# Feed-forward passes 1 to 9: the low parts of the weights move to GpSimd

## What is computed

```
f = rms_norm(h, ffn_norm_pre)
f = (silu(f @ w_gate) * (f @ w_up)) @ w_down      # w_gate, w_up: 2048 x 5632, w_down: 5632 x 2048
h = h + rms_norm(f, ffn_norm_post)
```

## Time and profile before

| | |
|---|---|
| median of three runs | 1993.66 us |
| span of the profiled execution, first to last instruction | 1992.0 us |
| time of the profiled execution beyond its span | not listed; 1.66 us lie between the span and the median |
| PE busy | 1979.0 us, 99% |
| PE weight load busy | 1681.0 us, 84% |
| DVE busy | 1668.8 us, 84% |
| ACT busy | 1147.6 us, 58% |
| POOL busy | 18.9 us, 1% |
| mean DMA rate | 198 GB/s |

### The profile page before, as it was taken

The page is one execution under the profiler, slowest core; times in us unless marked ns, Lnnn a source line. Parts: engine busy times, 40 slices in busy tenths (PEclk is TensorE's granted clock), DMA queues, the critical chain, the costliest instruction groups (busy, mean ns, idle before and its releaser), DMA issues.

```text
span 1992.0 us, 29428 instructions
## 1 busy us (share of the span) xinstructions
PE 1979.0 (99%) x10149; PEld 1681.0 (84%) x10149; DVE 1668.8 (84%) x2336; ACT 1147.6 (58%) x1482; POOL 18.9 (1%) x37
## 2 busy tenths in 40 slices
PE   9999999999999999999999999999999999999998
PEld 8888888888888888998888888888888888888886
DVE  7788888889888868767777787999999988888887
ACT  6666566666655545565545565556555555555575
POOL 0000000000000000000000000000000000000000
PEclk9999999999999999999999999999999999999999
DMA  8666676666566566545556667666566666766754
GB/s 235 200 191 190 190 206 184 188 192 195 172 207 209 189 203 223 156 132 156 191 191 239 205 207 242 189 202 202 190 201 200 200 201 201 254 201 207 244 189 152
DMA packets 255197, 394.74 MB, mean 198 GB/s; under 512 B 28840, under 2 KB 161440, under 8 KB 252928
## 3 DMA queue, kind: packets, MB, share of 16 engines
q1 hardware_dynamic: 251104, 369.87, 59.7%
q0 software_dynamic: 3824, 23.43, 3.5%
q10 hardware_dynamic: 176, 0.20, 0.0%
HBM read 387.08 MB, written 6.36 MB: 198 GB/s over the span
## 4 chain that ended last, share of the span: by engine, by line
PE 98%; DVE 1%; ACT 0%; DMA 0%; issue 0%; DVEq 0%; SPq 0%; ACTq 0%
PE acc L655 16%; PE acc L851 15%; PE acc L853 15%; PE acc L852 15%; PE acc L660 8%; PE acc L912 6%; PE acc L913 6%; PE acc L914 6%; PE acc L1107 1%; PE acc L785 1%; PE acc L637 1%; PE acc L636 1%; PE acc L638 1%; PE acc L1038 1%; PE acc L1242 0%; PE acc L714 0%
## 5 line engine op out<-in xcount | busy, mean ns | idle before, releaser
L1914 DVE TENSOR_TENSOR wlo<-raw,whi 128x1024 fp32r<-128x1024 f32 (+2 forms) x559 | 662.5, 1205 | 110.8 <-ACT whi L1351 108.3
L1351 ACT ACTIVATE whi<-raw 128x1024 fp32r<-128x1024 f32 (+1 forms) x560 | 572.2, 1044 | 244.4 <-PE acc L853 81.7
L655 PE MATMUL acc<-u,whi 128*128 128x512 f32 x1376 | 328.7, 391 | 0.0
L851 PE MATMUL acc<-whi,u 128*128 128x512 f32 x824 | 323.0, 392 | 0.1
L853 PE MATMUL acc<-whi,u 128*128 128x512 f32 x824 | 320.8, 389 | 0.0
L852 PE MATMUL acc<-wlo,u 128*128 128x512 f32 x824 | 320.6, 389 | 0.0
L655 PEld LDWEIGHTS acc<-u,whi 128*128 128x128 f32 x1376 | 252.7, 188 | 48.8
L851 PE MATMUL acc<-whi,g 128*128 128x512 f32 x520 | 202.8, 390 | 0.1
L853 PE MATMUL acc<-whi,g 128*128 128x512 f32 x520 | 202.4, 389 | 0.0
L852 PE MATMUL acc<-wlo,g 128*128 128x512 f32 x520 | 202.3, 389 | 0.0
L1374 ACT ACTIVATE whi<-raw 128x1024 fp32r<-128x1024 f32 x72 | 76.5, 1062 | 209.9 <-PE acc L914 162.0
(11 more groups left out here) (597 smaller groups left out, 2990.8 us busy)
## 6 DMA issues: line engine op xcount, KB each, us to landing
raw<-w_in_in SPq DMA_DIRECT2D x208, 512.0 KB, 3.8
raw<-w_gate_in SPq DMA_DIRECT2D x176, 256.0 KB, 3.0
raw<-w_up_in SPq DMA_DIRECT2D x176, 256.0 KB, 3.3
raw<-w_down_in SPq DMA_DIRECT2D x88, 512.0 KB, 4.6
raw<-w_ssm_o_in SPq DMA_DIRECT2D x64, 512.0 KB, 4.3
raw<-w_in_in SPq DMA_DIRECT2D x64, 256.0 KB, 4.0
raw<-w_attn_o_in SPq DMA_DIRECT2D x32, 512.0 KB, 4.7
raw<-w_out_in SPq DMA_DIRECT2D x32, 512.0 KB, 4.9
```

Source lines behind the costliest of these rows:

```text
L655: return T.matmul(bank(banks[i]), wh[:, j, i * P:i * P + P], src[:, kts[j], :, :].rearrange("p a s -> p (a s)"), start=start and j == 0, s ...
L851: T.matmul(o, x_hi, wh[:, j, :], start=start, stop=False, skip_group_check=True)
L1351: S.activation(whi[:, slot, 0:w], raw[:, slot, 0:w], ACT.Copy).then_inc(sem("hi_ready"), 1)
L1914: V.tensor_tensor(wlo[:, slot, 0:w], raw[:, slot, 0:w], whi[:, slot, 0:w].bitcast(F32), ALU.subtract) \
```

## The change

It touches passes 1 to 9 of `ff`.

- All low parts of raw weights are made by GpSimd (`raw_low`, `seven_raw_low`): one instruction of 128x1024 for a plain chunk, three of 128x512 for a pair, the first of which counts a new semaphore, `first_lo`. `lo_ready` is counted by GpSimd in these passes. At the end of pass 9 VectorE waits for the last of them before it makes the low parts of pass 10.
- VectorE does nothing for a plain chunk. For a pair (`pooled_sums`) it makes the three sum instructions and the two low parts of the sums.
- TensorE starts a pair at `first_lo`, waits for the second and third low part later, and does the product with the last raw block after two of the products with sums.
- ScalarE has two more waits ahead of the high parts of the sums (`t_used`, and one on `chunk_done` that applies only to adjacent pairs, of which this order has none). The high part of a `dn` operand moves from chunk 12 to chunk 1 of the next pass; on VectorE its sums move from chunk 11 to chunk 15, its low part from chunk 14 to chunk 1 of the next pass.
- SP waits for the sums too before it overwrites a slot of a pair, and its loads of all 11 passes are written out, with no loop.
- Several semaphores are merged under one name, in this phase and in others, with the same order of events. Lists for passes with four or five pairs are added and left empty.

```diff
+FF_FOURS = ()
+FF_FIVES = ()
+POOLED = tuple(("ff", _j) for _j in FF_THREES)
...
 # SP, load
                 sp.wait_ge(sem("lo_ready"), num(phase, it, c) - RING + 1)
+                if phase == "ff" and isinstance(it, int):
+                    it_, c_ = (it, c - RING) if c >= RING else (it - 1, c - RING + PHASES["ff"][0])
+                    if is_pooled("ff", it_) and is_seven("ff", it_, c_):
+                        n = SEVENS_BEFORE["ff", it_] + SEVEN["ff", it_].index(pair_of("ff", it_, c_))
+                        sp.wait_ge(sem("t_sum"), 3 * n + (3 if c_ % 2 else 1))
...
 # GpSimd, behind the store of h to h_dram
+        def raw_low(it, c):
+            slot = c % RING
+            pool.wait_ge(sem("hi_ready"), num("ff", it, c) + 1)
+            G.tensor_tensor(wlo[:, slot, :], raw[:, slot, :], whi[:, slot, :].bitcast(F32), ALU.subtract) \
+                .then_inc(sem("lo_ready"), 1)
+        def seven_raw_low(it, c):
+            slot = c % RING
+            pool.wait_ge(sem("hi_ready"), num("ff", it, c) + 1)
+            G.tensor_tensor(wlo[:, slot, 512:], raw[:, slot, 512:], whi[:, slot, 512:].bitcast(F32), ALU.subtract) \
+                .then_inc(sem("first_lo"), 1)
+            G.tensor_tensor(wlo[:, slot + 1, 0:512], raw[:, slot + 1, 0:512], whi[:, slot + 1, 0:512].bitcast(F32),
+                            ALU.subtract).then_inc(sem("lo_ready"), 1)
+            pool.wait_ge(sem("hi_ready"), num("ff", it, c + 1) + 1)
+            G.tensor_tensor(wlo[:, slot + 1, 512:], raw[:, slot + 1, 512:], whi[:, slot + 1, 512:].bitcast(F32),
+                            ALU.subtract).then_inc(sem("lo_ready"), 1)
+        pool.wait_ge(sem("lo_ready"), num("ff", FF_THREES[0], 0))
+        for it in FF_THREES:
+            for c_ in range(16):
+                if not is_seven("ff", it, c_):
+                    raw_low(it, c_)
+                elif c_ % 2 == 0:
+                    seven_raw_low(it, c_)
...
 # TensorE, seven_products
-            begin(phase, it, c + 1)
+            if pooled:
+                pe.wait_ge(sem("first_lo"), pooled_before(it, n) + 1)
+            else:
+                begin(phase, it, c + 1)
...
             product(v_bank(phase, it, 0), tokens(t0 + 2 * p, 0), weights(slot, 1), first, last)
-            product(c_bank(phase, it, 1, 0), tokens(t0 + 2 * p + 1, 0), weights(slot + 1, 1))
+            if pooled:
+                begin(phase, it, c)
+            else:
+                product(c_bank(phase, it, 1, 0), tokens(t0 + 2 * p + 1, 0), weights(slot + 1, 1))
...
+            if pooled:
+                begin(phase, it, c + 1)
+                product(c_bank(phase, it, 1, 0), tokens(t0 + 2 * p + 1, 0), weights(slot + 1, 1))
             pe.wait_ge(sem("t_lo"), 2 * done + 2)
...
 # VectorE
+        def sums_low(phase, it, n, half):
+            t, t_hi, t_lo = sums_at(phase, it), thi[phase], tlo[phase]
+            dve.wait_ge(sem("t_hi"), 2 * n + 1 + half)
+            two = slice(2 * half, 2 * half + 2)
+            V.tensor_tensor(t_lo[:, two, :], t[:, two, :], t_hi[:, two, :].bitcast(F32), ALU.subtract) \
+                .then_inc(sem("t_lo"), 1)
+        def pooled_sums(phase, it, c, between=None):
...
+            V.tensor_tensor(t[:, 0:2, :], raw_f[:, inner].rearrange("p (a n) -> p a n", a=2),
+                            raw[:, slot, 0:512].unsqueeze(1).to_broadcast([P, 2, 512]), ALU.add) \
+                .then_inc(sem("t_sum"), 1)
...
+            V.tensor_tensor(t[:, 2, :], t[:, 0, :], raw[:, slot + 1, 0:512], ALU.add).then_inc(sem("t_sum"), 1)
+            dve.wait_ge(sem("t_sum"), 3 * n + 2)
+            V.tensor_tensor(t[:, 3, :], t[:, 2, :], raw[:, slot + 1, 512:], ALU.add).then_inc(sem("t_sum"), 1)
+            if between:
+                between()
+            sums_low(phase, it, n, 0)
+            if not ahead:
+                sums_low(phase, it, n, 1)
...
-            if not is_seven(phase, it, c):
+            if is_pooled(phase, it):
+                if is_seven(phase, it, c) and c % 2 == 0:
+                    pooled_sums(phase, it, c, between)
+            elif not is_seven(phase, it, c):
                 split(phase, it, c)
```

More of the change, by code:

```diff
@@ L83 @@
 SEVEN["pg", 0] = (0, 1)
-SEVEN.update({("ff", _j): (0, 1, 2) if _j in FF_THREES else (0, 1) for _j in range(1, FF_LAST + 1)})
+SEVEN.update({("ff", _j): tuple(range(5 if _j in FF_FIVES else 4 if _j in FF_FOURS else 3 if _j in FF_THREES else 2))
+              for _j in range(1, FF_LAST + 1)})
 SEVEN.update({("dn", _j): (0, 1, 2, 3, 4, 5, 6, 7, 8) for _j in range(2)})
@@ L93, with pairs_in @@
 }
+PAIRS.update({("ff", _j): (5, 6, 0, 1, 2, 3, 4, 7) for _j in FF_FIVES})
+PAIRS.update({("ff", _j): (4, 5, 0, 1, 6, 2, 3, 7) for _j in FF_FOURS})
+def pairs_in(phase, it):
+    return PAIRS.get((phase, it), PAIRS[phase]) if isinstance(it, int) else PAIRS[phase]
 PAIRS_AT = {"so": 16, "ao": 16, "wo": 0, "ff": 0, "dn": 0, "pg": 0}
-MERGE = {_p: PAIRS_AT[_p[0]] + 2 * PAIRS[_p[0]].index(SEVEN[_p][-1]) + 2 for _p in PASSES}
+MERGE = {_p: PAIRS_AT[_p[0]] + 2 * pairs_in(*_p).index(SEVEN[_p][-1]) + 2 for _p in PASSES}
 SEVENS_BEFORE = {_p: sum(len(SEVEN[_q]) for _q in PASSES[:_i]) for _i, _p in enumerate(PASSES)}
@@ L140, in is_seven, with is_pooled, pooled_before @@
     return (phase, it) in PASSES and pair_of(phase, it, c) in SEVEN[phase, it]
+def is_pooled(phase, it):
+    return isinstance(it, int) and (phase, it) in POOLED
+def pooled_before(it, n):
+    return sum(len(SEVEN["ff", _j]) for _j in FF_THREES if _j < it) + n
 def num(phase, it, c):
@@ L295, in build, with sums_at @@
         s_u[ph] = at("s_u_" + ph, [P, 2, 512], hi_at)
+    ts_ff = at("ts_ff", [P, 4, 512], G0 + 32 * 2048)
+    def sums_at(phase, it):
+        return ts_ff if phase == "ff" and isinstance(it, int) and it in FF_APART else tr[phase]
     raw_f, whi_f, wlo_f = (w[:, :, :].rearrange("p r n -> p (r n)") for w in (raw, whi, wlo))
@@ L546, in _ @@
             first = 0
-            if its == 1 or phase in TURNS or phase == "ssm":
+            if its == 1 or phase == "ssm":
                 for c_ in range(per):
@@ L550, in _ @@
                 first = 1
-            if its > 1:
+            if phase == "ff":
+                for it_ in range(its):
+                    for c_ in range(per):
+                        load(it_, c_)
+            elif its > 1:
                 with sp.Fori(first, its) as it:
@@ L924, in seven_products @@
                 pe.wait_ge(sem("ff_lo"), FF_LAST + 1)
-            product(v_bank(phase, it, 3), differences(3) if phase in KEPT else tokens(2 * p, 1), sums(1), first, last)
+            product(v_bank(phase, it, 3), differences(3) if phase in KEPT else tokens(2 * p, 1), sums(1), first, last) \
+                .then_inc(sem("t_used"), 1)
+            if pooled:
+                begin(phase, it, c + 1)
+                product(c_bank(phase, it, 1, 0), tokens(t0 + 2 * p + 1, 0), weights(slot + 1, 1))
             pe.wait_ge(sem("t_lo"), 2 * done + 2)
@@ L1378, in seven_high @@
             for half in range(2):
+                if is_pooled(phase, it) and half == 0:
+                    act.wait_ge(sem("t_used"), n)
+                if is_pooled(phase, it) and half and is_seven(phase, it, c - 1):
+                    act.wait_ge(sem("chunk_done"), num(phase, it, c))
                 act.wait_ge(sem("t_sum"), 3 * n + 1 + 2 * half)
                 two = slice(2 * half, 2 * half + 2)
-                S.activation(thi[phase][:, two, :], tr[phase][:, two, :], ACT.Copy).then_inc(sem("t_hi"), 1)
+                S.activation(thi[phase][:, two, :], sums_at(phase, it)[:, two, :], ACT.Copy).then_inc(sem("t_hi"), 1)
         def wide_high(phase, it, c, between=None):
@@ L1809, in _ @@
                     ff_gate(it - 1)
[L1810 to L1811 removed]
+                if c_ == 1 and 2 <= it <= 5:
+                    operand_high(DN_OPERANDS + it - 2)
         act.wait_ge(sem("p_in"), 64)
@@ L2155, in tables @@
                     link(last)
-            last.then_inc(sem("gp_all"), 1)
-            dve.wait_ge(sem("gp_all"), 1)
+            link(last)
         def prepare_dt():
@@ L2773, in _ @@
                 seven_merged("ff", it, c_)
+                if c_ == 1 and 2 <= it <= 5:
+                    operand_low(DN_OPERANDS + it - 2)
                 if c_ == (1 if it - 1 in FF_THREES else 2):
@@ L2777, in _ @@
                     ff_product(it - 1)
-                if it <= 4 and c_ == 11:
+                if it <= 4 and c_ == 15:
                     operand_sums(DN_OPERANDS + it - 1)
-                if it <= 4 and c_ == 14:
-                    operand_low(DN_OPERANDS + it - 1)
+            if ("ff", it + 1) in PASSES and is_pooled("ff", it) and not is_pooled("ff", it + 1):
+                dve.wait_ge(sem("lo_ready"), num("ff", it + 1, 0))
         for it in range(2):
```

85 lines of the change are left out of this document (51 added, 34 removed).

## The result

The changed kernel takes 2064.6 us (median of four runs, 2063.57 to 2065.68) against 1993.62 us: 71 us more, a ratio of 1.0355 with an interval of 1.0341 to 1.037. That is slower, inside the stated range and 17 us above the forecast of 2048. The profiled execution has a span of 2061.9 us.

The account below looks back on a forecast made before the run. TensorE, busy 99% of the span, bounds the kernel; engines taking turns cost 9 x 6.0 = 54 us, giving a span of 2046 from 1992.0 and, with 1.7 us to the median, 2048 us; range 1991 to 2092 (8 in 10).

Parts of the forecast that it names:

- TensorE fills the passes, only lateness can cost: Passes 1 to 9: TensorE fills all 42.4 us; gain under 0.1 us a pass, loss only if a producer is late.
- GpSimd's price: GpSimd's subtractions: 2.27 us for 128x1024, 1.30 for 128x512, 34.4 us a pass, so GpSimd alone keeps up.
- Turns: GpSimd and two-SBUF-operand VectorE instructions take turns, so a pass holds their sum; 54 us in all, chance 0.48.
- 6.0 us a pass, as the sum of both engines' time less TensorE's: Passes 1 to 9: 34.4 + 15.1 = 49.5, 48.4 with overlapping ends, 6.0 us over TensorE's 42.4.
- The operand: "nothing": Later phase's operand work moved into the plain stretch: adds 3.05 us to GpSimd's 13.6 against 17.2, costing nothing.
- In the old place it would be 12 us: Operand work left among the pairs would cost 3 us a pass in four passes, 12 us.
- Clock stays 1.00: TensorE's granted clock was to stay at 1.00 in the changed kernel.
- No disturbance: Rival: GpSimd and VectorE run side by side, GpSimd always ahead; 1994 us, within 2 us; chance 0.30.
- GpSimd too slow: Rival: GpSimd alone takes 3.65 and 2.05 us, a pass 55 us; + 113, 2107 us; chance 0.08.
- Shared by the element: Rival: each engine slows the other a little, 0.5 to 2 us a pass; about 2005 us; chance 0.10.
- the lower part (1991 to 2020): Part of the 8-in-10 range below the forecast's own 2020 to 2085, there because no disturbance lies at 1994.
- The forecast's upper end: With GpSimd at 2.44 and 1.37 us, a pass takes 51.8 us and the loss is 9 x 9.4 = 85 us.

Follow-up runs that it names:

- m1_port: Small separate kernel computing nothing of the layer: staged GpSimd and VectorE instructions, alone and together; at 1024 elements from SBUF, both together took 3.3 us a pair.
- k2_tiny_sums: Changed kernel with the pairs' sums, their low and high parts cut to one column per block in passes 2 to 9; 2007.87 us, ratio 1.0069.
- k9_all_plain: Kernel before, with GpSimd making low parts of all ten plain chunks in passes 1 to 9, VectorE those of pairs; 2029.29 us, ratio 1.0174.
- k3_yield: Changed kernel with one more wait: GpSimd waits for both low parts of a pair's sums before the next plain chunk; 2063.75 us, ratio 1.0347.
- k4_operand_old: Changed kernel with all parts of the later phase's operand back at chunks 11, 12 and 14 of the same pass; 2054.54 us, ratio 1.0304.
- k5_later: Changed kernel with ScalarE's high part of the operand moved behind the high part of chunk 2; 2072.18 us, ratio 1.0394.
- k6_plain_stretch: Kernel before, with GpSimd making only the low parts of six plain chunks in a row (14, 15, 0 to 3); 1994.86 us, ratio 1.0006.

## Why the prediction was right

- **TensorE fills the passes, only lateness can cost.** Right: the growth of the nine periods is the whole loss, and the 17.9 us of VectorE's relief a pass brought nothing.
- **GpSimd's price.** The forecast took 2.27 and 1.30 us; alone it is 2.30 and 1.22 from start to start, which makes 34.0 us a pass against the 34.4 assumed.
- **Turns.** Right, as `m1_port` shows it directly and `k2_tiny_sums` shows it for this kernel. By the Trainium skill (SBUF — State Buffer, "Who interferes with whom") a VectorE instruction with two SBUF inputs contends with a GpSimd one that reads SBUF and not with one that only writes, and a VectorE instruction with at most one SBUF input, outside its two-port modes, does not contend. The runs agree in all three (3.3 us a pair; 1.218; 1.215 beside 2.353).
- **6.0 us a pass, as the sum of both engines' time less TensorE's.** Measured 5.7 where no operand is made. The size is right, the picture behind it less so, and that the two lie so close is partly luck: the two engines are not busy without gaps (GpSimd idles some 6 us of 48), and in `k9_all_plain` the same kind of sum gives 42.5 for a period of 45.1. The chain of five VectorE instructions in front of TensorE carries it, each with a GpSimd instruction let in ahead; `k3_yield` shows that taking turns out of the low parts puts one in ahead of the first sum.
- **The operand: "nothing". This is the step that failed,** and it accounts for most of the 17 us between forecast and result. Three periods took 4.4 to 4.5 us more than 48.1 and the two around them 2.5 and 2.6, 18.5 us in all (8.2 + 10.2 + 10.1 + 10.2 + 8.3 - 5 x 5.7 = 18.5). I summed the engines' time over the stretch and found room, where it is a relay on four in-order queues. The timeline of the changed kernel from chunk 15 of pass 3 to chunk 2 of pass 4 (VectorE, ScalarE, GpSimd, TensorE):
```profile
1384.81 2.50 DVE L2030 TENSOR_TENSOR xd_full<-xd_full 128x256 f32<-128x256 f32 x1
...
1388.13 0.85 ACT L1437 ACTIVATE xh<-xd_sum 128x768 fp32r<-128x768 f32 x1 [5.18 <-DVE xd_sum L2032]
...
1390.32 2.52 POOL L655 TENSOR_TENSOR wlo<-raw,whi 128x1024 fp32r<-128x1024 f32 x1 [3.29 <-ACT whi L1427]
...
1392.89 0.50 PE L916 MATMUL acc<-whi,u 128*128 128x512 f32 x1 [1.59 <-POOL wlo L655]
```
 A sum of 0.42 us waits 2.1 for its turn; ScalarE waits 5.2 us with the operand's high part, and the high part of chunk 2 stands behind it; GpSimd idles 3.3 us for that, and TensorE 1.6. The foldings come later too, and the next pass's first sum with them. That the place of the operand matters is shown (`k4_operand_old`); how the 18.5 us divide among these waits is not, since `k5_later` took away only ScalarE's hold of chunk 2 and became slower.
- **"In the old place it would be 12 us."** It is less: 2.2 us in each of four periods (`k4_operand_old`), 9 us, and the whole kernel 10 us faster than with the move. I had the sign of the move wrong.
- **Clock stays 1.00.** Not quite: it is 0.96 or 0.97 in three of nine periods. Each time TensorE had just waited 1.8 to 1.9 us for the sums' low parts, and the clock then lay at 0.50 for a few microseconds. In this kernel there is no time to show for it (48.09 us beside 48.08); in `k3_yield` the three periods that had it in their last pair were 0.8 to 1.0 us longer.
- **The rivals.** No disturbance, and GpSimd too slow, are both refuted. Shared by the element falls by the single-file pace. Of the range, the lower part (1991 to 2020) was held for a case that the stage with both engines excludes. The forecast's upper end was summed unevenly: 51.8 leaves out the 1.1 us of overlapping ends that 46.1 and 48.4 have taken off; with it the loss would be 9 x 8.3 = 75 us in place of 85, which still covers the 70 measured.

No version here beats the kernel before, and the reason is its first view: TensorE is full. What VectorE gains in `k6_plain_stretch`, 6.6 us a pass, could only pay as a fourth pair of seven products, 0.68 us less TensorE time a pass; this wasn't tried.

## What to carry to other kernels

Before work is given to GpSimd beside a busy VectorE, sort VectorE's instructions by where their operands lie: those with two in SBUF and a GpSimd subtraction go one by one, and in a dependent chain of short ones each link can pay one turn of GpSimd's. Give GpSimd the stretches in which VectorE reads PSUM; there 50 subtractions cost about 1 us in all. And a sum over a stretch says whether the work fits, not whether it comes in time: for each moved instruction that waits, follow what stands behind it on its own queue, one engine after the other, to the one that is full.

## What the runs showed that was not expected

Two engines with full queues alternate strictly, one instruction each, whatever their lengths: 3.3 us a pair for 1024 elements beside 1024, 2.7 for 1024 beside 512, 1.7 for 512 beside 512, each a little under the sum of the two alone; and a VectorE instruction of 0.42 us took 2.50. Delaying GpSimd on purpose won at most 0.6 us of 5.7 a period, and the three periods with TensorE's low-clock stretch in their last pair became longer than without the delay. A GpSimd memset of 128x1024 takes 0.95 us and disturbs nothing.
